# Delta rule of a fused two-block model: sums of squares from one fp32 matmul, or from two float32r matmuls over a square and its residue

## The reference, cut to what matters

```python
def _l2norm(x):
    return x * lax.rsqrt(jnp.sum(x * x, axis=-1, keepdims=True) + EPS)

def _rms(x, gain):
    xf = x.astype(jnp.float32)
    return xf * lax.rsqrt(jnp.mean(xf * xf, axis=-1, keepdims=True) + EPS) * gain.astype(jnp.float32)

# inside the chunked delta rule (64 tokens a chunk), with k_beta = k * beta:
L = jnp.where(strict, jnp.einsum("bhncd,bhnsd->bhncs", k_beta, k) * decay, 0.0)
a_mat = L + jnp.eye(CHUNK, dtype=f32)
sol = lax.linalg.triangular_solve(a_mat, rhs, left_side=True, lower=True, unit_diagonal=True)
attn = jnp.where(tril, jnp.einsum("bhncd,bhnsd->bhncs", q, k) * decay, 0.0)
```

## Time and profile before

| | |
|---|---|
| time, three runs | 813.09 us median, 811.12 to 813.42 |
| the profiled execution | 808.39 us, of which the span from first to last instruction is 806.6 us |
| granted TensorE clock, mean | 0.998 of full |
| stretch of the delta rule | about 467 us (first `d_sq`) to 634 us |

### The profile page before, as it was taken

How to read it: one execution, slowest core, us unless ns; L and a number is a source line. 1 busy time by engine, 2 the same in 40 slices (tenths; PEclk the granted TensorE clock), 3 DMA queues, 4 the chain that set the end, 5 groups by cost and what they waited for, 6 DMA issues and landing times.

```text
span 806.6 us, 16232 instructions
## 1 busy us (share of the span) xinstructions
PE 774.5 (96%) x6694; PEld 716.6 (89%) x6694; DVE 666.0 (83%) x1349; ACT 493.2 (61%) x1018; POOL 0.2 (0%) x4
## 2 busy tenths in 40 slices
PE   9999999999999999999999988999999899989998
PEld 8888899999999999999888867898888889778898
DVE  6699989896788888888897977878787779978775
ACT  6688555454546666665547476365826467577882
POOL 0000000000000000000000000000000000000000
PEclk9999999999999999999999999999999999999999
DMA  8744646758464566564766342321333347744411
GB/s 339 319 157 147 227 155 255 280 196 306 160 200 166 195 226 234 183 212 160 304 262 263 111 152 106 106 96 63 106 138 126 105 150 267 278 180 177 152 53 54
DMA packets 23402, 148.48 MB, mean 184 GB/s; under 512 B 2848, under 2 KB 3488, under 8 KB 7328
## 3 DMA queue, kind: packets, MB, share of 16 engines
q1 hardware_dynamic: 22752, 146.39, 50.4%
q10 hardware_dynamic: 576, 1.05, 0.4%
HBM read 146.38 MB, written 1.05 MB: 183 GB/s over the span
## 4 chain that ended last, share of the span: by engine, by line
PE 69%; DVE 18%; ACT 9%; issue 2%; DMA 1%; ACTq 0%; DVEq 0%
PE ps L2250 52%; PE ps L2237 4%; DVE wlo L1636 4%; ACT whi L1227 1%; DVE mqk L1633 1%; DVE raw L1659 1%; DVE kT L1633 1%; ACT L1204 1%; DMA x<-xT 1%; DVE qT L1633 1%; PE pp L2461 1%; PE pp L2438 1%; DVE x L1633 1%; PE pp L2501 1%; DVE tmp L1633 1%
## 5 line engine op out<-in xcount | busy, mean ns | idle before, releaser
L1636 DVE TENSOR_TENSOR wlo<-raw,whi 128x512 fp32r<-128x512 f32 (+2 forms) x436 | 276.5, 660 | 13.8 <-ACT whi L1227 13.2
L1227 ACT ACTIVATE whi<-raw 128x512 fp32r<-128x512 f32 (+2 forms) x436 | 239.5, 601 | 3.0 <-DMA raw<-wst 2.8
L2250 PE MATMUL ps<-p0hi,whi 128*128 128x256 f32 x1136 | 190.7, 290 | 1.6 <-ACT p0hi L1285 0.7
L2250 PE MATMUL ps<-p0hi,wlo 128*128 128x256 f32 x1136 | 181.5, 281 | 4.2 <-DVE wlo L1636 3.9
L2250 PE MATMUL ps<-p0lo,whi 128*128 128x256 f32 x1136 | 180.7, 281 | 0.2
L2250 PEld LDWEIGHTS ps<-p0hi,whi 128*128 128x128 f32 x1136 | 155.8, 189 | 10.1 <-issue 5.8
L2250 PEld LDWEIGHTS ps<-p0hi,wlo 128*128 128x128 f32 x1136 | 153.7, 188 | 6.6 <-DVE wlo L1636 6.4
L2250 PEld LDWEIGHTS ps<-p0lo,whi 128*128 128x128 f32 x1136 | 154.3, 189 | 1.0 <-DVE p0lo L1636 0.8
L1659 DVE CUSTOM_DVE_ANT_0 raw<-raw,cact,vc 128x1024 f32<-128x1024 f32 x64 | 81.8, 1279 | 0.0
L2237 PE MATMUL ps<-zz,whi 128*128 128x512 f32 x154 | 44.7, 393 | 0.0
L1204 ACT ACT_TABLE_LOAD x22 | 28.2, 1283 | 9.0 <-DVE smo L1787 6.0
(11 more groups left out here) (387 smaller groups left out, 1205.4 us busy)
## 6 DMA issues: line engine op xcount, KB each, us to landing
raw<-wst SPq DMA_DIRECT2D x124, 1024.0 KB, 5.1
raw<-wsd SPq DMA_DIRECT2D x16, 704.0 KB, 4.6
x<-xT ACTq DMA_DIRECT2D x4, 256.0 KB, 5.2
raw<-wst SPq DMA_DIRECT2D x4, 256.0 KB, 6.0
m_x<-memT SPq DMA_DIRECT2D x1, 1024.0 KB, 14.6
outT<-x SPq DMA_DIRECT2D x3, 256.0 KB, 2.3
cact<-cB SPq DMA_DIRECT2D x1, 512.0 KB, 14.0
cst<-con SPq DMA_DIRECT2D x1, 364.0 KB, 11.5
```

Source lines behind the costliest of these rows:

```text
L1227: act.activation(whi[n % NHL][:, a:b], raw[k % NRAW][:, a:b], ACT.Copy).then_inc(*tick("hi"))
L1636: return v.tensor_tensor(lo, src, hi.bitcast(F32), ALU.subtract)
L2250: ins = t.matmul(o, l, r, start=begins and k0 == 0 and half == "hh" and c == 0 and (q == 0 or twice), stop=ends and not more and half == t ...
```

## The change

Each square is now taken twice on ScalarE: once rounded to float32r (`d_sh`, `d_osh`) and once in fp32 as before (`d_sq`, `d_osq`). VectorE subtracts the first from the second and rounds the residue to float32r (`d_sl`, `d_osl`). TensorE sums the two terms with two float32r matmuls that accumulate in one bank; the ones matrix is now a float32r column that is broadcast (`plus`). The first of the two waits for the rounded square, the second for the residue. Two entries of `HOLD` are added: in group 3 `d_ktp` and `d_kt` stand one part earlier. The diff, cut to its core:

```diff
+    ('gdn', 21, 3): 1, ... ('gdn', 3, 3): 0,
...
             for n in range(2):
+                add("d_sh", i, n)
                 add("d_sq", i, n)
+                add("d_sl", i, n)
             yield from pause("gdn", 0, i)
...
             add("d_o", i)
+            add("d_osh", i)
             add("d_osq", i)
+            add("d_osl", i)
             yield from pause("gdn", 12, i)
...
+        def dh(n_, n):
+            return flat(tmpr[:, 4 + 2 * (n_ % 2):6 + 2 * (n_ % 2), :]) if n else trr[3 * (n_ % 2) + 2]
...
+                elif kind == "d_sh":
+                    n_, n = i
+                    e.wait_ge(*on("gsilu", n_))
+                    if n_ >= 2:
+                        e.wait_ge(*on("d_oones", n_ - 2))
+                        e.wait_ge(*on("d_on", n_ - 2))
+                    v = flat((kT if n else qT)[:, 2 * n_:2 * n_ + 2, :])
+                    act.activation(dh(n_, n), v, ACT.Square).then_inc(*tick("d_sh"))
...
+                elif kind == "d_osh":
+                    n_, = i
+                    e.wait_ge(*on("d_o", n_))
+                    act.activation(flat(kTr[:, 2 * n_:2 * n_ + 2, :]), ps[3 + 2 * (n_ % 2)], ACT.Square).then_inc(*tick("d_osh"))
...
+                elif kind == "d_sl":
+                    n_, n = i
+                    t = tr[3 * (n_ % 2) + n]
+                    e.wait_ge(*on("d_sq", n_, n))
+                    low(trr[3 * (n_ % 2) + n], t, dh(n_, n)).then_inc(*tick("d_sl"))
...
+                elif kind == "d_osl":
+                    n_, = i
+                    t = tr[3 * (n_ % 2)]
+                    e.wait_ge(*on("d_osq", n_))
+                    low(trr[3 * (n_ % 2)], t, flat(kTr[:, 2 * n_:2 * n_ + 2, :])).then_inc(*tick("d_osl"))
...
                 elif kind == "d_ones":
                     n_, n = i
-                    e.wait_ge(*on("d_sq", n_, n))
+                    e.wait_ge(*on("d_sh", n_, n))
...
-                    t.matmul(ps[3 + 2 * (n_ % 2) + n], ones, tr[3 * (n_ % 2) + n], start=True, stop=True).then_inc(*tick("d_ones"))
+                    bank = ps[3 + 2 * (n_ % 2) + n]
+                    t.matmul(bank, plus, dh(n_, n), start=True, stop=False)
+                    e.wait_ge(*on("d_sl", n_, n))
+                    t.matmul(bank, plus, trr[3 * (n_ % 2) + n], start=False, stop=True).then_inc(*tick("d_ones"))
...
                 elif kind == "d_oones":
-                    e.wait_ge(*on("d_osq", n_))
+                    e.wait_ge(*on("d_osh", n_))
...
+                    t.matmul(bank, plus, flat(kTr[:, 2 * n_:2 * n_ + 2, :])[:, cut], start=True, stop=False)
+                    e.wait_ge(*on("d_osl", n_))
+                    t.matmul(bank, plus, trr[3 * (n_ % 2)][:, cut], start=False, stop=True).then_inc(*tick("d_oones"))
```

More of the change, by code:

```diff
@@ L198 @@
     "d_sq": "gdn_act", "d_rs": "gdn_act", "d_dexp": "gdn_act", "d_t0": "gdn_act", "d_v0c": "gdn_act",
-    "d_qexp": "gdn_act", "d_v1c": "gdn_act", "d_osq": "gdn_act", "d_ors": "gdn_act", "d_ohi": "gdn_act",
-    "d_nrm": "gdn_dve", "d_vb": "gdn_dve", "d_kt": "gdn_dve", "d_am": "gdn_dve", "d_u0": "gdn_dve",
+    "d_qexp": "gdn_act", "d_v1c": "gdn_act", "d_osq": "gdn_act", "d_osh": "gdn_act", "d_osl": "gdn_dve", "d_ors": "gdn_act", "d_ohi": "gdn_act",
+    "d_nrm": "gdn_dve", "d_sh": "gdn_act", "d_sl": "gdn_dve", "d_vb": "gdn_dve", "d_kt": "gdn_dve", "d_am": "gdn_dve", "d_u0": "gdn_dve",
     "d_xm": "gdn_dve", "d_u": "gdn_dve", "d_sc": "gdn_dve", "d_qs": "gdn_dve",
@@ L218 @@
     ('gdn', 0, 2): 0, ('gdn', 16, 0): 3, ('gdn', 16, 1): 1, ('gdn', 16, 2): 0, ('gdn', 20, 0): 1, ('gdn', 21, 2): 1,
[L219 to L226, removed]
@@ L227 @@
-    ('window', 1, 0): 3, ('window', 1, 3): 2, ('window', 2, 0): 0, ('window', 2, 1): 0, ('window', 20, 0, 1): 1,
-    ('window', 20, 3, 0): 1, ('window', 20, 3, 1): 1, ('window', 3, 1): 2, ('window', 4, 0): 2, ('window', 4, 2): 0,
-    ('window', 6, 2): 1, ('window', 6, 3): 2,
+    ('gdn', 21, 3): 1, ('gdn', 22, 0): 1, ('gdn', 22, 3): 0, ('gdn', 23, 3): 1, ('gdn', 3, 3): 0, ('gdn', 5, 2, 1): 2,
+    ('gdn', 5, 2, 3): 1, ('gdn', 6, 2, 3): 2, ('gdn', 6, 2, 5): 0, ('gdn', 6, 3, 6): 1, ('gdn', 9, 2): 2, ('gdn_gates', 1): 0,
@@ new lines @@
+    ('gdn_gates', 2): 2, ('head', 0, 'k', 0): 2, ('head', 0, 'k', 1): 2, ('head', 0, 'k', 2): 2, ('head', 0, 'k', 3): 2,
+    ('head', 0, 'q', 0): 2, ('head', 0, 'q', 1): 2, ('head', 0, 'q', 2): 1, ('head', 0, 'q', 3): 2, ('head', 20, 'k', 3): 1,
+    ('head', 20, 'q', 2): 1, ('mem_norm', 3): 2, ('mlstm', 0, 0): 0, ('mlstm', 0, 2): 2, ('mlstm', 1, 0): 2, ('mlstm', 1, 2): 2,
+    ('mlstm', 1, 3): 0, ('mlstm', 2, 3): 2, ('mlstm', 20, 2): 1, ('mlstm', 21, 3): 1, ('stick', 0, 0): 0, ('stick', 0, 2): 0,
@@ new lines @@
+    ('stick', 0, 3): 0, ('stick', 20, 0, 1): 1, ('stick', 20, 1, 0): 1, ('stick', 20, 3, 0): 1, ('stick', 20, 4, 0): 1,
+    ('stick', 20, 7, 0): 1, ('stick', 20, 7, 1): 2, ('stick', 3, 1): 0, ('stick', 4, 0): 5, ('stick', 4, 1): 2,
+    ('stick', 4, 2): 2, ('stick', 4, 5): 0, ('window', 0, 1): 2, ('window', 1, 0): 3, ('window', 1, 3): 2, ('window', 2, 0): 0,
+    ('window', 2, 1): 0, ('window', 20, 0, 1): 1, ('window', 20, 3, 0): 1, ('window', 20, 3, 1): 1, ('window', 3, 1): 2,
+    ('window', 4, 0): 2, ('window', 4, 2): 0, ('window', 6, 2): 1, ('window', 6, 3): 2,
@@ L1509, in _ @@
                     t = tr[3 * (n_ % 2) + n]
-                    e.wait_ge(*on("gsilu", n_))
                     if n_ == 1:
@@ L1558, in _ @@
                     act.activation(flat(Xm[n_ % 2][:, 2:4, :]), ps[4 + 2 * (n_ % 2)][:, 0:T], ACT.Copy).then_inc(*tick("d_v1c"))
+                elif kind == "d_osh":
+                    n_, = i
+                    e.wait_ge(*on("d_o", n_))
+                    act.activation(flat(kTr[:, 2 * n_:2 * n_ + 2, :]), ps[3 + 2 * (n_ % 2)], ACT.Square).then_inc(*tick("d_osh"))
                 elif kind == "d_osq":
                     n_, = i
-                    e.wait_ge(*on("d_o", n_))
                     act.activation(tr[3 * (n_ % 2)], ps[3 + 2 * (n_ % 2)], ACT.Square).then_inc(*tick("d_osq"))
@@ L2591, in _ @@
                     n_, *m = i
-                    e.wait_ge(*on("d_osq", n_))
+                    cut = slice(m[0] * T, (m[0] + 1) * T) if m else slice(0, 2 * T)
+                    bank = ps[6 - 2 * m[0]][:, 0:T] if m else ps[4 + 2 * (n_ % 2)]
+                    e.wait_ge(*on("d_osh", n_))
                     if m:
                         e.wait_ge(*on("d_ors", 2))
-                        t.matmul(ps[6 - 2 * m[0]][:, 0:T], ones, tr[3][:, m[0] * T:(m[0] + 1) * T], start=True, stop=True).then_inc(*tick("d_oones"))
-                    else:
-                        t.matmul(ps[4 + 2 * (n_ % 2)], ones, tr[3 * (n_ % 2)], start=True, stop=True).then_inc(*tick("d_oones"))
+                    t.matmul(bank, plus, flat(kTr[:, 2 * n_:2 * n_ + 2, :])[:, cut], start=True, stop=False)
+                    e.wait_ge(*on("d_osl", n_))
+                    t.matmul(bank, plus, trr[3 * (n_ % 2)][:, cut], start=False, stop=True).then_inc(*tick("d_oones"))
                 elif kind == "h_ones":
```

## The result

| | before | changed |
|---|---|---|
| median of six runs on one chip | 810.76 us (808.55 to 813.42) | 817.46 us (816.24 to 820.74) |
| profiled execution | 808.39 us | 820.74 us |

The ratio is 1.0086, with a 95% interval of 1.0069 to 1.0103: 7.0 us slower (0.86% of 810.76 us; the two medians lie 6.7 us apart), where the forecast added 4.4. The forecast time of 817.5 us is met to 0.04 us, but 2.3 us of that is luck: it stood on 813.09 us, the median of three runs of the kernel before, and six runs give 810.76. What has to be explained is +7.0, not 817.46.

The account below looks back on a forecast made before the run. The prediction took ScalarE as the chain at entries 0, 1 and 3, despite TensorE's 96%. Entries 3.3 and 0.2, exits 0.4, 0, 0.5, 0 gave +4.4 us on 813.09: 817.5 us, range 811.5 to 820.

Parts of the forecast that it names:

- What bounds the stretch: 467 to 632 us: ScalarE holds the chain at entries 0, 1, 3; old sums hold it only at entry 2 and exits.
- Entries 0, 1 and 3: Group entries 0, 1, 3: two more squares lengthen the ScalarE chain, 1.1 us each, 3.3 us in all.
- Entry 2: Entry of group 2: TensorE's saving goes into the wait for the residue, +0.2 us, bounds -0.4 and +0.7.
- Exits: Exits 0 to 3: square and residue delay VectorE; +0.4, 0 (beside entry 3's ScalarE chain), +0.5 and 0 us.
- `HOLD`: Group 3, d_ktp a part earlier: taken as nothing, though it may keep up to 0.5 us from being lost.
- The sum: Whole change: 3.3 + 0.2 + 0.4 + 0 + 0.5 + 0 = +4.4 us, nothing but the start changing outside 467 to 634 us.
- The clock, 0: Whole kernel: the forecast itself kept the clock as before, adding nothing for it, at a chance of 0.50.
- The rival: Entry 1: TensorE's clock falls, a part takes twice as long while d_dec waits; +1.4 us on top, 818.9 us, chance 0.18.
- First square to `d_vtp`: Sign at entry 0: this step should grow from 6.24 us to about 7.3 us.
- To `d_nrm` of k at entry 1: Sign at entry 1: the step from the first square to d_nrm should grow from 5.6 to 6.7 us.
- VectorE idle ahead of residues: Sign in the changed kernel: VectorE should show idle time ahead of its residues, released by ScalarE; no size given.
- TensorE's busy time: Sign over the changed kernel: TensorE's busy time should fall by near 5 us and its idle time rise by 9.

Follow-up runs that it names:

- `rounded_only`: Changed kernel without fp32 square, residue and second matmul, so each sum is one float32r matmul and lacks its low term; 809.38 us, ratio 0.9981 against before.
- `hold_old`: Changed kernel with the old HOLD table, so d_ktp of group 3 stands where it did; 818.40 us, ratio 1.0093 against the kernel before.
- `filler`: Changed kernel with idle matmuls on TensorE at entries 0 and 1 while it waits for square and residue; 817.61 us, ratio 1.0080 against before.
- `act_squares`: Kernel before with q and k squared once more on ScalarE at each entry, results unread, sums still fp32, no residue; 813.96 us, ratio 1.0048.
- `entries_only`: Changed kernel with the exits put back to one square and the fp32 sum; 816.60 us, ratio 1.0076 against the kernel before.
- `exits_only`: Changed kernel with the entries put back to one square each and fp32 sums; 814.10 us, ratio 1.0047 against the kernel before.
- `dve_square`: As `entries_only`, but VectorE makes the fp32 square at the entries as a product; 815.89 us, ratio 1.0066 against the kernel before.
- `late_residues`: Changed kernel with all residues, at entries and exits, moved behind the pause; 825.12 us, ratio 1.0165 against the kernel before.
- `exits_late`: As `exits_only`, with the exit residue d_osl moved behind a part of weight matmuls; 817.53 us, ratio 1.0069 against the kernel before.
- `exit_squares`: Kernel before with one more ScalarE square at each exit, result unread, fp32 sums, no residue; 812.54 us, ratio 1.0018.
- `before_filler`: Kernel before with idle matmuls on TensorE at entries 0 and 1 while it waits for the square; 811.98 us, ratio 1.0001.

## Why the prediction was right, and where its size was off

- **What bounds the stretch.** Right. TensorE's 96% was no reason for a gain: `rounded_only` has the least TensorE work of all and gains nothing at entries 0 and 1, as read from the earlier trace rows.
- **Entries 0, 1 and 3, 1.1 us each.** Right as a mechanism and in size: 1.02 (`hold_old`), 1.03 (`filler`) and 1.15 (`act_squares`), and `act_squares` shows that it is ScalarE's squares. For entries 0 and 1 these are the numbers with the clock back in time.
- **Entry 2, +0.2.** 0.54, by the difference of two kernels, and 0.55 in `entries_only`, inside the bounds.
- **Exits, +0.4, 0, +0.5, 0.** 0.37, 0.30, 0.64 and 0.24 (`exits_only`). The zero at exit 1 was wrong: the 0.30 are there with entry 3 as before. In the changed kernel exit 1 and entry 3 cost 0.87, less than entry 3's squares alone, so the two do run side by side, as I wrote, and a little of TensorE's saving may show.
- **`HOLD`, 0.** Right: 818.40 us without the move, 818.90 with it.
- **The sum.** Without the clock: 1.02 + 1.03 + 0.91 + 0.87 + 0.62 + 0.24 = 4.7 us, forecast 4.4.
- **The clock, 0.** This is the step that failed: "the forecast itself, with the clock as before". Its part in the stretch is 1.75 at entry 0 and 1.0 at entry 1, 2.7 us; another 2.0 us lie behind 636 us, where I had taken that nothing changes. The rival had the mechanism for entry 1 (less work, a wait in between, a part at half clock with `d_dec` behind it) at a chance of 0.18 and a price of 1.4; it measured 1.0. I had not asked the question at entry 0, where the clock was low already: for 3.4 us in the kernel before, for 10.3 us in the changed one, into the stretch where the chain is on TensorE. 4.7 + 2.7 = 7.4 us is the sum of the table.
- **Is it the change, or chance?** At entry 1 it is the change: a low stretch begins between 499 and 507 us in the six traces with the float32r pair, its residue and no filler (the changed kernel twice, `hold_old`, `entries_only`, `dve_square`, `late_residues`), and in none of the others, among them `act_squares` (squares without the pair) and `rounded_only` (less work, no wait for a residue, 2.79 of 4 us busy). So neither the shorter sum nor the later square alone brought it about, one trace of each; that it takes the shorter sum together with the wait is my reading.
- **The same at entry 0.** Partly chance: a low stretch lies there in every trace, and one of 3 to 4 us costs between nothing and 1.6 us by when it begins; only kernels with residues at the entries had it for more than 6 us.
- **The same behind 636 us.** The 2.0 us go with the changed exits. Each of the eight traces with float32r sums at the exits has one low stretch that begins between 620 and 655 us: five at 642 to 652 (the changed kernel twice, `exits_only`, `exits_late` and `rounded_only`, 2.0 to 2.2 us each), three at 623 to 629 instead (`hold_old`, `filler`, `late_residues`), which have nothing from 636 to 663 us and more at exit 2 (`hold_old` has one more at 719 us, for another 2.1). None of the six with the exits' sums as before (the kernel before, `act_squares`, `entries_only`, `dve_square`, `exit_squares`, `before_filler`) has one between 560 us and the end of the program, though TensorE was busy for as little as 1.68 of 4 us there. The order of `HOLD` is not it, since `entries_only` has the new one and `hold_old` the old. What in the changed exits brings it about stays open.
- **From 7.4 to 7.0.** The table compares with the profiled execution of before, 2.4 us under its median of six. With the 2.0 behind 636 us, the changed kernel comes to 9.4 us above that execution, and 9.4 - 2.4 = 7.0. That the two agree to the tenth is chance (the table is worked out from single executions). What the other executions of before lose to the position of a low stretch, and what to the slower TensorE between 247 and 370 us, is open: with a mean clock of 0.998 in each, those of the first set took between 808.43 and 812.39 us.
- **The signs.** First square to `d_vtp` 7.28 for 7.3: right. To `d_nrm` of k at entry 1 7.71 for 6.7: 1.0 off, the clock. VectorE idle ahead of residues, released by ScalarE: right. TensorE's busy time should fall by 5 us and rose by 6.6, its idle time rose by 5.7 (37.8 after, 32.1 before) instead of 9: with up to 9.0 us more of lost clock inside the busy time, the fall would be some 2.4 us. This sign was blind to the clock and tested nothing.

## What to carry to other kernels

Work taken from an engine that is busy for 96% of the span pays only where the chain holds that very work; ask at each place which engine ends last, since 12 shorter sums (`rounded_only`) saved 2.9 us in the five places that waited for them and nothing at the others, and two squares on the 61% engine cost 1.0 us wherever ScalarE was the chain. When an edit makes TensorE's work shorter and puts a wait into it, price the next part of matmuls at half clock too, at each place where the busy time ahead is already low. A few tenths of a per cent between two profiled executions can be the position of one low-clock stretch: compare medians, and follow single instructions through several traces before believing a place.

## What the runs showed of the hardware that I had not expected

- A low stretch of the clock cost nothing at 468.9 to 472.3 us (before) and 1.4 us at 474.6 to 478.0 (`exit_squares`), in code that is the same up to there. In two executions of the same changed kernel the low stretches stood at the same instructions; with two entries of `HOLD` different, which moved no work ahead of 586 us, they stood at others (1.02 us for entry 0 instead of 2.77).
- The granted clock does not tell all of TensorE's pace. Between 300 and 310 us it was 1.00 and TensorE busy throughout in both traces, yet the window has 88 matmul records in the kernel before and 86 in the changed one, in equal code. From 247 to 360 us the same instructions lie 2.6 us further apart in the changed one; the second execution of the changed kernel has none of it. The cause is open.
- Keeping TensorE busy in the waits of two entries raised the mean clock from 0.987 to 0.994 but gave back only 1.3 us of the median; low stretches appeared in other places. The Trainium skill, "TensorE: Matmul & The Clock Gate", section "What's actually happening", says that the throttled state is the default and activity releases it. Entry 1 of `filler` fits this: 3.89 of 4 us busy, and the clock stayed at 1.00 where it fell in the changed kernel.
- A square from PSUM or SBUF costs ScalarE the same whether it writes fp32 or float32r (steps of 0.50 to 0.54 us, records of 0.59 to 0.63).
